# Attention scores from high and low parts in two fp32r products, exponents in a ring of three

## What is computed

```python
def fox_attend(q, k, v, f_q, f_k, q_pos, k_pos):
    s = jnp.einsum('bqhd,bkhd->bhqk', q, k, preferred_element_type=jnp.float32)
    s = s + jnp.swapaxes(f_q, 1, 2)[..., :, None] - jnp.swapaxes(f_k, 1, 2)[..., None, :]
    s = jnp.where(k_pos[None, :] <= q_pos[:, None], s, -1e30)
    p = jax.nn.softmax(s, axis=-1)
    return jnp.einsum('bhqk,bkhd->bqhd', p.astype(v.dtype), v)
```

## Time and profile before

| | |
|---|---|
| median of 3 runs | 2926.5 us (2924.05 to 2928.64) |
| profiled execution, its own time | 2922.55 us |
| its span in the trace | 2920.7 us |
| PE busy | 2813.4 us, 96% of the span, 16931 instructions |
| DVE, ACT, POOL busy | 1307.9, 530.9, 883.9 us |
| mean granted PE clock | 0.987 of full |
| attention stage | about 384 to 720 us |

### The profile page before, as it was taken

The page is one execution under the profiler, slowest core; times in us unless marked ns, Lnnn a source line. Parts: engine busy times, 40 slices in busy tenths (PEclk is TensorE's granted clock), DMA queues, the critical chain, the costliest instruction groups (busy, mean ns, idle before and its releaser), DMA issues.

```text
span 2920.7 us, 42681 instructions
## 1 busy us (share of the span) xinstructions
PE 2813.4 (96%) x16931; PEld 2498.8 (86%) x16931; DVE 1307.9 (45%) x2088; ACT 530.9 (18%) x829; POOL 883.9 (30%) x490
## 2 busy tenths in 40 slices
PE   5999989999999999999999999999899999999998
PEld 3899954445899999999999899954899999999998
DVE  3116755554354343444356303156454444434445
ACT  4200012323041010100101413134241010010100
POOL 2322235443222322333323322200324333243330
PEclk9999999999999999999999999999999999999999
DMA  7411267775512322223211322141301111111111
GB/s 313 123 44 37 59 202 234 217 213 152 210 37 101 101 73 90 84 82 107 66 37 44 103 63 103 51 147 55 118 30 56 45 44 46 41 50 38 55 43 58
DMA packets 208126, 275.37 MB, mean 94 GB/s; under 512 B 10742, under 2 KB 152713, under 8 KB 201068
## 3 DMA queue, kind: packets, MB, share of 16 engines
q1 hardware_dynamic: 204812, 255.89, 27.6%
q10 hardware_dynamic: 3024, 16.88, 1.5%
q0 software_dynamic: 144, 0.52, 0.0%
HBM read 245.24 MB, written 28.04 MB: 94 GB/s over the span
## 4 chain that ended last, share of the span: by engine, by line
PE 90%; DVE 4%; issue 2%; ACT 2%; SPq 1%; DMA 1%; POOL 0%; DVEq 0%; ACTq 0%
PE ps L855 69%; PE ps L873 4%; PE ps L841 2%; PE ps L1151 2%; PE ps L1136 2%; PE ps L1111 2%; PE ps L997 1%; PE ps L1178 1%; DVE xT L1856 1%; PE ps L1305 1%; PE ps L904 1%; PE ps L1294 1%; PE ps L1333 1%; PE ps L1312 1%; DMA ada_late<-in_w_ada_dram 1%
## 5 line engine op out<-in xcount | busy, mean ns | idle before, releaser
L756 POOL CAST whi<-stage 128x1024 fp32r<-128x1024 f32 x194 | 207.9, 1072 | 1770.5 <-PE ps L855 1298.5
L855 PE MATMUL ps<-hh,whi 128*128 128x344 f32 x2832 | 607.7, 323 | 5.7 <-issue 2.0
L855 PE MATMUL ps<-hl,whi 128*128 128x344 f32 x2832 | 601.6, 321 | 0.0
L855 PE MATMUL ps<-hh,wlo 128*128 128x344 f32 x2832 | 598.0, 319 | 0.0
L757 POOL TENSOR_TENSOR wlo<-stage,whi 128x1024 fp32r<-128x1024 f32 x194 | 519.4, 2677 | 15.5
L855 PEld LDWEIGHTS ps<-hh,whi 128*128 128x128 f32 x2832 | 474.4, 188 | 26.1 <-issue 24.6
L855 PEld LDWEIGHTS ps<-hl,whi 128*128 128x128 f32 x2832 | 479.5, 189 | 0.0
L855 PEld LDWEIGHTS ps<-hh,wlo 128*128 128x128 f32 x2832 | 472.1, 188 | 0.0
L855 PE MATMUL ps<-hid_hi,whi 128*128 128x344 f32 x1536 | 330.4, 323 | 10.7 <-DVE xT L1856 10.7
L855 PE MATMUL ps<-hid_lo,whi 128*128 128x344 f32 x1536 | 326.6, 321 | 0.0
L855 PE MATMUL ps<-hid_hi,wlo 128*128 128x344 f32 x1536 | 324.8, 320 | 0.0
(11 more groups left out here) (331 smaller groups left out, 2477.7 us busy)
## 6 DMA issues: line engine op xcount, KB each, us to landing
stage<-in_w_ff_dram SPq DMA_DIRECT2D x128, 512.0 KB, 3.9
kpages<-in_cache_k_dram SPq DMA_DIRECT2D x128, 256.0 KB, 3.1
vpages<-in_cache_v_dram SPq DMA_DIRECT2D x128, 256.0 KB, 3.0
ada_late<-in_w_ada_dram SPq DMA_DIRECT2D x32, 1024.0 KB, 5.2
stage<-in_w_in_even_dram SPq DMA_DIRECT2D x25, 512.0 KB, 3.9
stage<-in_w_in_odd_dram SPq DMA_DIRECT2D x25, 512.0 KB, 3.9
xstore<-xT ACTq DMA_DIRECT2D x2, 4128.0 KB, 12.6
xT<-xstore SPq DMA_DIRECT2D x2, 4128.0 KB, 12.5
```

Source lines behind the costliest of these rows:

```text
L756: link(pool.tensor_copy(whi[:, u.c % 4, :], stage[:, u.c % 2, :]))
L855: last = pe.matmul(ps[:, 3 * t.par + c, 0:CH], w, x[:, c * CH:(c + 1) * CH], start=(k == 0 and q == 0), stop=(k == n - 1 and q == 2))
```

## The change

In pass one and two each fp32 product becomes two fp32r products into the same bank. The first multiplies the rounded (high) parts of q and k, with extra rows of `negF` and of the shift in high and low part; the second has 128 rows, with the high part of q and the low part of k in one half, the low part of q and the high part of k in the other (`qhl`, `klh`). The product of the two low parts is left out. ACT writes the high parts a second time, into `klh` and `qhl`; DVE writes the low ones, as the difference of PSUM and the rounded copy. `PT` shrinks from a head's whole scores to a ring of three pieces, `exponent` n waits for `weighted` n - 3, and `a_av` now counts every piece. The semaphore `xt_done` gets a second use and a new name. SP has a wait for the scores of head 6 ahead of the first weight load behind the attention.

```diff
-        PT = at("PT", [P, NB * (NB + 1) // 2 * P], F32, B0)
-        qT = [at(f"qT{i}", [HD + 2, SEQ], F32, B0 + 18432 + 4096 * i) for i in range(2)]
-        kT = [at("kT0", [HD + 2, SEQ], F32, B0 + 26624), at("kT1", [HD + 2, SEQ], F32, W0 + 8192 + 4096 * KSLOTS)]
+        PT = at("PT", [P, 3, 512], F32, B0)
+        qT = [at(f"qT{i}", [HD + 4, SEQ], F32R, o) for i, o in enumerate((W0 + 4096, B0 + 6144))]
+        kT = [at(f"kT{i}", [HD + 4, SEQ], F32R, o) for i, o in enumerate((B0 + 10240, W0 + 8192 + 4096 * KSLOTS))]
+        qhl = [at(f"qhl{i}", [P, SEQ], F32R, B0 + 14336 + 4096 * i) for i in range(2)]
+        klh = [at(f"klh{i}", [P, SEQ], F32R, B0 + 22528 + 4096 * i) for i in range(2)]
...
+            sp.wait_ge(a_st, NP * (NH - 1))
             load_unit(V(U_OUT[0]), woe[:, :, 0:P])
...
                 if p:
-                    pool.wait_ge(a_av, 4 * p)
+                    pool.wait_ge(a_av, NP * 2 * p)
...
                 if c == 1:
-                    pe.wait_ge(a_k, 2 * g + 1)
+                    pe.wait_ge(a_k, 4 * g + 1)
+                    pe.wait_ge(xt_done_or_lows, lows(4 * g + 1))
...
                 if p == 0:
-                    pe.wait_ge(a_k, 2 * g + 2)
-                    pe.wait_ge(a_q, 2 * g + 2)
+                    pe.wait_ge(a_k, 4 * g + 4)
+                    pe.wait_ge(a_q, 4 * g + 4)
+                    pe.wait_ge(xt_done_or_lows, lows(4 * g + 4))
...
-                last = pe.matmul(o, qT[g % 2][0:HD + 1, i * P:(i + 1) * P], kT[g % 2][0:HD + 1, lo:lo + w],
-                                 start=True, stop=not diag)
+                pe.matmul(o, qT[g % 2][0:HD + 2, i * P:(i + 1) * P], kT[g % 2][0:HD + 2, lo:lo + w], start=True, stop=False)
+                last = pe.matmul(o, qhl[g % 2][:, i * P:(i + 1) * P], klh[g % 2][:, lo:lo + w], start=False, stop=not diag)
...
-                last = pe.matmul(o, kT[h % 2][0:HD + 2, j * P:(j + 1) * P], qT[h % 2][0:HD + 2, lo:lo + w],
-                                 start=True, stop=not diag)
+                pe.matmul(o, kT[h % 2][0:HD + 4, j * P:(j + 1) * P], qT[h % 2][0:HD + 4, lo:lo + w], start=True, stop=False)
+                last = pe.matmul(o, klh[h % 2][:, j * P:(j + 1) * P], qhl[h % 2][:, lo:lo + w], start=False, stop=not diag)
...
-                                 PT[:, key_at[j] + lo - j * P:key_at[j] + lo - j * P + w],
-                                 start=(j == 0), stop=(j == 4 * c + 3))
-                if p == head_end[c]:
-                    last.then_inc(a_av, 1)
+                                 PT[:, (NP * h + p) % 3, 0:w], start=(j == 0), stop=(j == 4 * c + 3))
+                last.then_inc(a_av, 1)
...
-                act.activation(kT[g % 2][0:HD + 1, 512 * c:512 * c + 512], ps[0:HD + 1, RING[c], :], ACT.Copy).then_inc(a_k, 1)
+                cols = slice(512 * c, 512 * c + 512)
+                act.activation(kT[g % 2][0:HD + 2, cols], ps[0:HD + 2, RING[c], :], ACT.Copy).then_inc(a_k, 1)
+                act.wait_ge(a_k, 4 * g + 2 * c + 1)
+                act.activation(klh[g % 2][HD:P, cols], kT[g % 2][0:HD, cols].bitcast(F32), ACT.Copy).then_inc(a_k, 1)
...
-                act.activation(qT[g % 2][0:HD, 512 * c:512 * c + 512], ps[0:HD, RING[(2 + c) % 3], :], ACT.Copy).then_inc(a_q, 1)
+                cols = slice(512 * c, 512 * c + 512)
+                act.activation(qT[g % 2][0:HD, cols], ps[0:HD, RING[(2 + c) % 3], :], ACT.Copy).then_inc(a_q, 1)
+                act.wait_ge(a_q, 4 * g + 2 * c + 1)
+                act.activation(qhl[g % 2][0:HD, cols], qT[g % 2][0:HD, cols].bitcast(F32), ACT.Copy).then_inc(a_q, 1)
...
-                o = key_at[j] + lo - j * P
-                act.activation(PT[:, o:o + w], ps[:, 4 + p % 2, 0:w], ACT.Exp).then_inc(a_p, 1)
+                n = NP * h + p
+                if n >= 3:
+                    act.wait_ge(a_av, n - 2)
+                act.activation(PT[:, n % 3, 0:w], ps[:, 4 + p % 2, 0:w], ACT.Exp).then_inc(a_p, 1)
...
+            def key_lows(g, c):
+                dve.wait_ge(a_k, 4 * g + 2 * c + 1)
+                cols = slice(512 * c, 512 * c + 512)
+                tt(klh[g % 2][0:HD, cols], ps[0:HD, RING[c], :], kT[g % 2][0:HD, cols].bitcast(F32), ALU.subtract
+                   ).then_inc(xt_done_or_lows, 1)
+
+            def query_lows(g, c):
+                dve.wait_ge(a_q, 4 * g + 2 * c + 1)
+                cols = slice(512 * c, 512 * c + 512)
+                tt(qhl[g % 2][HD:P, cols], ps[0:HD, RING[(2 + c) % 3], :], qT[g % 2][0:HD, cols].bitcast(F32), ALU.subtract
+                   ).then_inc(xt_done_or_lows, 1)
...
                 if more:
                     key_scores(8 * g)
+                    for c in range(2):
+                        key_lows(g, c)
+                    for c in range(2):
+                        query_lows(g, c)
                 sequence_top(h)
```

More of the change, by code:

```diff
@@ L162, in build @@
         lft = put("lft", [P, NB + 1, NH])
-        negF = put("negF", [P, NB, NH])
-        QS = put("QS", [P, NB, 2])
+        negF = put("negF", [P, NB, NH, 2], F32R)
+        QS = put("QS", [P, NB, 4], F32R)
         prevT = put("prevT", [P, 4, 16])
@@ L295, in build @@
         ada_kept = sem("ada_kept")
-        xt_done = sem("xt_done")
+        xt_done_or_lows = sem("xt_done_or_lows")
         xt_kept = sem("xt_kept")
@@ L448, in multiplied, with lows @@
             return n // 2 + 1 if n < PAGES // 2 else n - 3
-        key_at = [sum(SEQ - m * P for m in range(j)) for j in range(NB)]
+        def lows(n):
+            return KT + n
         def all_read(eng, t):
@@ L504, in _ @@
                 load_unit(V(U_IN[0] + i), wie[:, :, 1536 + i * P:1536 + (i + 1) * P])
-            sp.wait_ge(xt_done, KT)
+            sp.wait_ge(xt_done_or_lows, KT)
             for k in range(KT):
@@ L785, in attention @@
                 for x in (kT[0], qT[0], kT[1], qT[1]):
-                    pool.memset(x[HD:HD + 2, :], 1.0).then_inc(a_rows, 1)
+                    pool.memset(x[HD:HD + 4, :].bitcast(F32), 1.0).then_inc(a_rows, 1)
                 pool.wait_ge(a_rows, 4)
@@ L990, in _ @@
                                 xin[:, b, k * P:(k + 1) * P])
-                last.then_inc(xt_done, 1)
+                last.then_inc(xt_done_or_lows, 1)
             pe.wait_ge(setup_dve, 3)
@@ L1085, in keys_turned @@
                     turn(o[0:HD, :], QK[:, 1, b, g * HD:(g + 1) * HD])
-                    last = pe.matmul(o[HD:HD + 1, :], negF[:, b, g:g + 1], ident[:, :], start=True, stop=True)
+                    last = pe.matmul(o[HD:HD + 2, :], negF[:, b, g, :].bitcast(F32), ident[:, :], start=True, stop=True)
                 last.then_inc(a_tk, 1)
@@ L1122, in shift_turned @@
                 for b in range(4 * c, 4 * c + 4):
-                    last = pe.matmul(ps[HD:HD + 2, bank, (b % 4) * P:(b % 4 + 1) * P], QS[:, b, :], ident[:, :],
+                    last = pe.matmul(ps[HD:HD + 4, bank, (b % 4) * P:(b % 4 + 1) * P], QS[:, b, :].bitcast(F32), ident[:, :],
                                      start=True, stop=True)
@@ L1509, in _ @@
             for k in range(KT):
-                act.wait_ge(xt_done, k + 1)
+                act.wait_ge(xt_done_or_lows, k + 1)
                 act.activation(xT[:, k, NS:T].rearrange("p (a n) -> p a n", a=2),
@@ L1588, in denominator @@
                 r = rden[rows, 512 * c:512 * c + 512]
-                act.wait_ge(a_av, 2 * h + c + 1)
+                act.wait_ge(a_av, NP * h + head_end[c] + 1)
                 if h == 0 and c == 0:
@@ L2067, in samples_normed @@
                 dve.wait_ge(prep_pe, PE_STEP["f_summed"])
-                link(dve.tensor_scalar(negF[:, :, :], ps[:, 6, 0:NB * NH].rearrange("p (b h) -> p b h", h=NH), -1.0, None, ALU.mult))
+                F = ps[:, 6, 0:NB * NH].rearrange("p (b h) -> p b h", h=NH)
+                link(dve.tensor_scalar(negF[:, :, :, 0], F, -1.0, None, ALU.mult))
+                link(stt(out=negF[:, :, :, 1], in0=F, scalar=-1.0, in1=negF[:, :, :, 0].bitcast(F32), op0=ALU.mult,
+                         op1=ALU.subtract))
             dve.wait_ge(setup_pe, 2)
-            dve.memset(QS[:, :, 0], 1.0)
+            dve.memset(QS[:, :, 0:2].bitcast(F32), 1.0)
             dve.memset(sc[:, :, PAGES, :], NEG)
@@ L2146, in shift @@
                     dve.wait_ge(a_again, 2 * g)
-                dve.tensor_scalar(QS[:, :, 1], peak[:, :], -1.0, None, ALU.mult).then_inc(a_shift, 1)
+                link(dve.tensor_scalar(QS[:, :, 2], peak[:, :], -1.0, None, ALU.mult))
+                stt(out=QS[:, :, 3], in0=peak[:, :], scalar=-1.0, in1=QS[:, :, 2].bitcast(F32), op0=ALU.mult, op1=ALU.subtract
+                    ).then_inc(a_shift, 1)
+            def key_lows(g, c):
[8 more added lines that the diff above has]
+                   ).then_inc(xt_done_or_lows, 1)
             def normed(h, c):
@@ L2188, in head @@
                 sequence_masked(h)
+            for c in range(2):
+                key_lows(0, c)
+            for c in range(2):
```

(1 more changed line is left out.)

2 lines of the change are left out of this document (1 added, 1 removed).

## The result

The changed kernel takes 2917.57 us (median of 6 runs, 2911.33 to 2928.52), the kernel before in the same session 2926.81 us (6 runs, 2924.05 to 2930.87). The ratio is 0.9968, interval 0.9956 to 0.9981: faster, by 9.2 us. The forecast was 26.8 us, and the measured time lies above the range's upper end of 2911. The profiled execution of after is the fastest of its six, 2911.33 us with a span of 2909.6.

The account below looks back on a forecast made before the run. TensorE was taken to bound each attention head. Seven heads at 4.7 us (32.9) plus 3.0 in the last gave 35.9 us; less 9.1 for the clock, 26.8, so 2926.5 becomes 2899.7 us, range 2888 to 2911.

Parts of the forecast that it names:

- the product's price: Score products in both passes: two fp32r cost 0.93 ns a column against 1.78 for one fp32, saving 7.8 us a head.
- the clock: TensorE's clock falls once a head behind its waits for ScalarE, costing 1.3 us in each of seven heads, 9.1 us.
- the waits for exponents: TensorE's idle before the first two weighted products of a head: 1.5 and 2.4 us, against 0.4 and 0.8 before.
- ScalarE's copies: Three second writes of 0.63 us each ahead of exponents 0 and 1 lengthen TensorE's path by 1.9 us a head.
- the waits of 1.2 us: Second-pass savings ahead of the sequence's output product and first two weighted products turn into waits: 1.2 us a head.
- the doubt that I kept for the range: The 128-column pieces may gain nothing from two products: 0.4 us less a head, 3 us over eight heads.
- The last head: Nothing is prepared there, so no extra ScalarE copies: 3.0 us saved (0 to 3.9).
- Lows on VectorE: Four subtractions a head, 2.7 us in all, fall where VectorE waits for keys: nothing on the path.
- SyncE as a floor of 36.0 us: SyncE's queue needs 36.04 us from head to head, so no head but the first gets below 36.0.
- The ring of three: Exponent n waits for weighted product n-3, whose slot has long been read: no cost.
- The first head: TensorE waits 7.3 us for VectorE's shift before head 0, so 3.9 us saved there count 0 (1.5 lost to 1.5 won).
- The slower rival: TensorE stays at the low clock for much of each head, 14 us a head: 2940 us; chance 0.05.

Follow-up runs that it names:

- kernel with fill and moved product: Changed kernel with unread fp32 products in TensorE's waits for exponents 0 and 1, and the sequence's output product behind the first weighted piece: 2902.39 us, ratio 0.9913.
- the run with one fp32 product: Changed kernel with all copies, low parts and ring, but one fp32 product for each fp32r pair in both passes: 2991.17 us, ratio 1.0224 to the kernel before.
- the run with one product less: Changed kernel with the second product of every piece left out in both passes, all preparation kept: 2929.21 us, ratio 1.0009 to the kernel before.

## Why the prediction was wrong

The forecast of 26.8 us was 35.9 less 9.1. The kernel with fill and moved product shows the changed kernel's attention at full clock: heads of 37.73, six of 36.60 and 24.97, 282.3 us, so 28.3 us less than before, where the sum said 35.9. Of the 17.6 us between forecast and result, then, 7.6 are missing at full clock, some 7 are the clock's (16 where I had 9.1), and some 3 lie behind the attention. Two terms of the sum failed about equally, the product's price and the clock; the waits for exponents came close to the forecast.

- **ScalarE's copies, 1.9 us a head, and the waits of 1.2 us: right.** The waits are 1.39 and 2.20 us, 2.8 us more than before where the sum had 3.1, and the second copies take 0.63 us. The 0.72 us that I took from the Trainium skill (ScalarE: Activation LUTs, Rules for kernel authors) is too high for them: the row there is for an instruction with a bias operand, which these copies don't have.
- **The product's price, 0.93 ns a column for two: too low, the first term that failed.** From 512.19 to 512.66 a pair of 512 columns takes 0.47 us, as I had it, but that pair follows an fp32r product. Behind a mask, as from 517.79 to 518.10, the first product takes 0.31 us and not 0.23. I had read the price from rows in which nothing but fp32r products follow one another; here 18 of head 2's 24 pairs stand behind a mask or an fp32 product. The piece of 128 columns takes 0.24 us (512.66 to 512.90, mask included) against 0.28 before, where my price gives 0.18 and the doubt that I kept for the range 0.28: most of the doubt was right. Head 2 is 3.81 us shorter than before with 2.8 us more of waits, so its products gave 6.6 us and not 7.8. Heads 1 to 6 save 3.86 us at full clock, not 4.7: 5 us in all. The last head gives 1.5 (2.4 in the changed kernel) where I had 3.0, and head 0 3.7.
- **The clock, 1.3 us a head: the second, and the step whose idea failed.** I priced one short fall, from a single place. For heads 3 to 6 that is what came (37.7 to 38.3 against 36.65). But I took the clock as a fixed toll, once a head, from waits that I knew. It is not: the fall starts at one of three waits or doesn't come at all, ends after 3, 10 or 40 us, and while it lasts it can shift the other waits. All heads of the profiled run together lose 295.4 - 282.3 = 13.1 us against full clock, and that run is the fastest of six. The six runs' mean clocks go from 0.979 (2911.33 us) to 0.974 (2928.52 us). With 1 less the clock times the span as an estimate of the time lost, that is 61 and 76 us: 15 of the 17 us between them.
- **Lows on VectorE, nothing on the path: right for the four subtractions.** What I left out is the mask. I had `sequence_out` 0.14 us behind it and took that wait for fixed, but VectorE's steps in front of the mask are held by GpSimd, whose stream doesn't shorten with the head. The second operation of the shift, which I didn't cost at all, takes 2.29 us where GpSimd multiplies; but the one operation of before was held too, 1.87 us at the same place and up to 2.34, and I had not asked why. What the second one costs by itself no profile here shows.
- **SyncE as a floor of 36.0 us: wrong.** Heads of 34.5 us are possible for six heads in a row; the queue's lag is felt only at the end. Behind the attention I had nothing, and 3.65 us were given back.
- **The ring of three: right. The first head: right within 0.5 us at its start.** The slower rival had a chance of 0.05, with a reason against it that the run with one fp32 product disproved, and in the run with one product less nothing of the gain was left; it should have had more, and so should the range's upper end.

A version with the change's full arithmetic and two edits of order, ScalarE's second copies and the sequence's output product, beats both kernels: 2897.0 us, ratio 0.9898 to the kernel before.

## What to carry to other kernels

When a change makes TensorE's work shorter, list the waits that it opens on TensorE, and remove or fill those before counting the gain: here 16 us of 25 hung on waits of 1 to 2.2 us, and less work without that was no gain at all. Look in the trace of before for short operations whose longest duration is ten times the median: they are harmless while the engine has time, and become the path when the stage shrinks. A queue that is 1.5 us a head slower than the rest doesn't set the pace of a few heads, but it can come due at the end of the stage.

## What the runs showed of the hardware

- Waits of TensorE of 1.00 and 1.91 us, 2.7 us of products apart, were followed by 40 us at 1.2 GHz with TensorE busy throughout; after the same waits in other heads of that execution the clock was back within a few microseconds or stayed full (43.4 to 44.3 us and 42.58). The Trainium skill (TensorE: Matmul & The Clock Gate, Why this matters for your kernels) warns of long idle gaps between bursts of products. Here waits of 1 to 2.2 us were enough, so this trace asks for more care than the page does.
- In the changed kernel's head 2 an fp32r product of 512 columns takes 0.23 us, from its start to that of the next, behind another fp32r product, and 0.31 to 0.34 us behind a bf16 or fp32 one.
- A held VectorE operation needn't have two SBUF inputs. The shift's single `tensor_scalar` with an fp32 result reached 2.34 us in the kernel before, L2120 above 2.32 us, and both end 0.02 to 0.03 us behind a multiply. The one with an fp32r result stays at 0.23 us or less, but that doesn't show it free: in the changed kernel it starts only 0.2 us before a multiply's end in each of the three heads where GpSimd multiplies, takes 0.21 to 0.23 us there against 0.17 to 0.18 elsewhere, and ends 0.03 us behind the multiply. The Trainium skill (SBUF — State Buffer, Who interferes with whom) has `tensor_scalar` contend with GpSimd in its two-port modes, and this trace agrees.
- A page load whose address comes from a table takes SyncE 17.10 / 16 = 1.07 us, one with a fixed address 0.54 us.
